# Two scan directions added before one product: ScalarE takes the backward differences, VectorE the sum

## The chip, the cores and the metric

The kernel runs on one core of one Trainium2 chip. The metric is device time in microseconds (us) of one execution, lower is better. The kernel before took 1656.18 us (median of 3 runs, 1655.77 to 1656.74).

## What is computed

A two-layer encoder trunk over 512 positions of width 1024, batch 1, all in float32. Each layer makes one wide projection of the normed input, feeds three mixers (dilated attention, a bidirectional Mamba-2 scan, a short gated convolution), projects their outputs back, and ends in a convolutional feed-forward part. The change touches the scan alone. For one head (16 of them) and one chunk of 128 positions (4 of them) its part within the chunk is, cut to what matters:

```python
a_cs  = cumsum(dt * a)                      # along the chunk
decay = exp(where(lower, a_cs[l] - a_cs[s], -inf))
cb    = einsum(C[l], B[s])                  # shared by the 8 heads of a group
y_diag = (cb * decay) @ (xs * dt)           # 128 x 128 times 128 x 64
y = y_fwd + flip(y_bwd) + d_skip * xs       # two directions, each with its own dt and a
```

The forward direction looks at earlier positions (s <= l), the backward one at later positions, and both use the same B, C and xs.

## The kernel before, in words

**Weights.** All large products go through one stream of weight chunks of 128 x 1024 (list CHUNKS). A chunk is loaded by SyncE (SP) into one of two buffers, split on ScalarE into a rounded high part (`w_high`, L528), and the remainder, the low part, is made by VectorE during the scans (`low_after` of VectorE, L834) or by GpSimd elsewhere (L433). TensorE multiplies high x high, high x low and low x high (L1158 to L1160), 24 products of 512 columns for one tile. The chunk two places further on can be split only when TensorE has used this one, and loaded only when the one before it in the same buffer is split.

**Slots.** While the scans run, each layer steps through 28 slots (list SLOTS, L69): 12 tiles of the short convolution, 8 gate tiles z, 8 tiles of the output projection (o1). Every engine has its own in-order queue, written out by hand with the same loop over the slots, and semaphores tie the queues together. The scans hang on slots by tables: the 16 heads form two groups of 8, the groups begin at slots 2 and 13 (GROUP_AT), SEG_AT says in which slot a head's differences are taken, WEIGH_AT in which it is weighed, PAIR_AT in which a pair of heads (t = 0 to 7, 4 in each group) is multiplied.

**One head.** SP loads the running sums of both directions, spread over all 128 partitions, as one 128 x 2 x 512 tile (`head_rows`, L361; four buffers in turn, called sb_e (two of them), sb_e_third and sb_squares). VectorE subtracts the other position's sum from each chunk and direction and caps at 80: eight instructions of 128 x 128 (`seg`, L905). The column that is subtracted already has ln(dt) in it (L1033). ScalarE takes one Exp over all 128 x 1024 (`head_exp`, L602). VectorE multiplies by the masked products of C and B, which lie in PSUM, 128 x 1024 (`weigh`, L911). For even heads GpSimd adds the two directions, 128 x 512 (`add_directions`, L464).

**One pair.** After the tile of its slot TensorE multiplies the states (`from_states`, L1336, 12 products) and then, in `within` (L1322), takes three products a chunk: one for the even head's sum, two for the odd head's directions, accumulated. The even head writes partitions 0 to 63 of a bank, the odd head 64 to 127. Each float32 product appears as two instructions, so a pair has 24. VectorE's `combine` (L915 to L923) reads them, with the rows that SP's `pair_exps` (L370) loads, and GpSimd adds the backward part (L468) and gates (L473).

**Order around the change.** In a slot VectorE does: `seg`, state work, the tile's own evacuation, `weigh`, `low_after`, `combine`, the rest. ScalarE does `head_exp` before its `w_high` where the head's number within its group is 3 or more, else after it. GpSimd does state scaling, `add_directions`, `add_backward` (L468), gates. SP issues a slot's weight load, then a head's rows, which wait for the products of the pair that used the buffer, then a pair's exps. From slot 18 on, two stretches on ScalarE hold an activation-table change each way around a SiLU (`gate_silu`, L609, L610).

Of the kernel before, what the change touches and what calls it, by code (L numbers as in the profile page):

```python
# [9 lines left out]
ACT, ALU = mybir.ActivationFunctionType, mybir.AluOpType  # L10
P = 128
# [6 lines left out]
SSD_HEADS, SSD_GROUPS = 16, 2  # L18
# [5 lines left out]
QT = SEQ // P  # L24
# [3 lines left out]
DIR = 32  # L28
# [114 lines left out]
def build_trunk(nc, a):  # L143
# [18 lines left out]
    def sem(name, per=0):  # L162
        return Count(ctx.enter_context(nc.semaphore(name)), per, now)
# [16 lines left out]
    SM = sb("small", [P, 4, QT * 64])  # L180
# [51 lines left out]
    def bank(i):  # L232
# [41 lines left out]
    tok_tr, tok_copied = sem("tok_tr", 10), sem("tok_copied", 10)  # L274
    sin_first = sem("sin_first", 4)
    cb_mm, cb_done, xs_done, st_mm, sin_done = sem("cb_mm", 2), sem("cb_done", 4), sem("xs_done", 12), sem("st_mm", 12), sem("sin_done", 8)
    seg_done, e_done, g_done, y_mm = (
        sem(n, SSD_HEADS) for n in ("seg_done", "e_done", "g_done", "y_mm"))
    gs_done = sem("gs_done", SSD_HEADS // 2)
    yo_mm, y_read, t_read, z_copied, y_comb = (sem(n, 8) for n in ("yo_mm", "y_read", "t_read", "z_copied", "y_comb"))  # L280
    z_done = sem("z_done", 2)
    ff_tap, ff_silu, ff_hi, ff_lo = sem("ff_tap", 2 * FF_T), sem("ff_silu_done", FF_T), sem("ff_hi_done", FF_T), sem("ff_lo_done", FF_T)
# [8 lines left out]
    def head_e(h):  # L291

        return HEAD_E[h % 4]
# [9 lines left out]
    def column(d, h):  # L303
        return d * DIR + h
# [120 lines left out]
    def _(pool):  # L425
        g = nc.gpsimd
# [31 lines left out]
            g.tensor_tensor(SQ[:, j % 2, :].rearrange("p (h e) -> p h e", e=64), XT[:, c, :].rearrange("p (h e) -> p h e", e=64),  # L458
                            WS[:, c, col:col + 8].unsqueeze(2).to_broadcast([P, 8, 64]), ALU.mult).then_inc(xs_done.handle, 1)

        def add_directions(h):

            pool.wait_ge(*g_done.at(h + 1))
            g.tensor_tensor(head_e(h)[:, 0, :], head_e(h)[:, 0, :], head_e(h)[:, 1, :], ALU.add).then_inc(gs_done.handle, 1)  # L464

        def add_backward(t):
            pool.wait_ge(*y_read.at(t + 1))
            g.tensor_tensor(XC[:, t, 0:SEQ - P], XC[:, t, 0:SEQ - P], T[:, 1, 0:SEQ - P], ALU.add).then_inc(t_read.handle, 1)  # L468
# [8 lines left out]
        for layer in range(DEPTH):  # L477
            now[0] = layer
            for pos in range(POS["sc", 0]):
                low_after(*CHUNKS[pos])  # L480
                if layer == 0 and CHUNKS[pos] == ("qk", 2):
                    pool.wait_ge(bias_row.handle, 2)
                    g.dma_start(scratch[:, :, :], rm["bias_row"][:, :].unsqueeze(1).to_broadcast([HEADS, COPIES, REL]))\
                        .then_inc(bias_stored.handle, 16)
            for s, (kind, i) in enumerate(SLOTS):
                if kind == "sc" and i % 3 == 2:
                    t = i // 3
                    pool.wait_ge(*sc_hi.at(t + 1))
                    g.tensor_tensor(rm["ml_sc"][:, t, :], SCP[:, :], rm["mh_sc"][:, t, :].bitcast(F32), ALU.subtract)\
                        .then_inc(sc_lo.handle, 1)  # L490
                for grp in range(SSD_GROUPS):
                    if 0 <= s - GROUP_AT[grp] < 3:
                        for j in range(2):
                            scale_states(6 * grp + 2 * (s - GROUP_AT[grp]) + j)
                if s in WEIGH_AT and WEIGH_AT[s] % 2 == 0:
                    add_directions(WEIGH_AT[s])
                if s in PAIR_AT:
                    add_backward(PAIR_AT[s])
                if s in (16, 17):
                    gate(2 * (s - 16))  # L500
                    gate(2 * (s - 16) + 1)
                if s in (20, 21, 22):
                    gate(s - 16)
                if s == 24:
                    gate(7)
                if s in (24, 27):
                    sum_squares((s - 24) // 3)
            for m in range(KT):
                low_after("o2", m)
            for j in range(2 * FF_T):  # L510
                low_after("up", j)
                if j % 2 == 1:
                    t = j // 2
                    pool.wait_ge(*ff_hi.at(t + 1))
                    g.tensor_tensor(FLO[:, t, :], FP[:, :], FHI[:, t, :].bitcast(F32), ALU.subtract).then_inc(ff_lo.handle, 1)  # L515
            for i in range(DOWN_C * KT):
                low_after("dn", i)

    @block.scalar
    def _(act):  # L520
# [77 lines left out]
            sc.activation(PTS[:, u % 4, :, :], bank(4 + u % 2).rearrange("p (j i) -> p j i", i=P), ACT.Copy).then_inc(at_ptc.handle, 1)  # L598

        def head_exp(h):  # L600
            act.wait_ge(*seg_done.at(h + 1))
            sc.activation(head_e(h), head_e(h), ACT.Exp).then_inc(e_done.handle, 1)  # L602

        def gate_silu(last):

# [188 lines left out]
    def _(dve):  # L794
# [34 lines left out]
        def low_after(kind, i):  # L829

            n = now[0] * NCH + POS[kind, i] + 2
            dve.wait_ge(w_hi.handle, n + 1)
            dve.wait_ge(w_lo.handle, n)
            v.tensor_tensor(WLO[:, n % 2, :], W[:, n % 2, :], WHI[:, n % 2, :].bitcast(F32), ALU.subtract).then_inc(w_lo.handle, 1)  # L834
# [64 lines left out]
        def seg(h):  # L899
            dve.wait_ge(*rows_landed[h % 4].at(16 * (h // 4 + 1)))  # L900

            for d in range(2):
                for c in range(QT):
                    at = slice(P * c, P * c + P)
                    ins = v.tensor_scalar(head_e(h)[:, d, at], head_e(h)[:, d, at], AS[:, c, column(d, h):column(d, h) + 1], 80.0,  # L905
                                          ALU.subtract, ALU.min)
            ins.then_inc(seg_done.handle, 1)

        def weigh(h):
            dve.wait_ge(*e_done.at(h + 1))  # L910
            v.tensor_tensor(head_e(h), head_e(h), CB[:, :, :], ALU.mult).then_inc(g_done.handle, 1)  # L911

        def combine(t):
            dve.wait_ge(*y_mm.at(2 * t + 2))
# [27 lines left out]
        for layer in range(DEPTH):  # L942
# [81 lines left out]
            for s, (kind, i) in enumerate(SLOTS):  # L1024
# [4 lines left out]
                if s == 1:  # L1029
                    dve.wait_ge(*cs_tr.at(1))  # L1030
                    dve.wait_ge(*lndt_done.at(1))
                    for d in range(2):
                        step(v.tensor_tensor(AS[:, :, DIR * d:DIR * d + DIR], BANK[:, 3, P * d:P * d + P].rearrange("p (c n) -> p c n", n=DIR),  # L1033
                                             SM[:, 2, :].rearrange("p (c n) -> p c n", n=64)[:, :, DIR * d:DIR * d + DIR], ALU.subtract))
                    dve.sem_inc(cs_col.handle, 1)
                if s in SEG_AT:
                    seg(SEG_AT[s])
                for grp in range(SSD_GROUPS):
# [27 lines left out]
                if s in WEIGH_AT:  # L1066
                    weigh(WEIGH_AT[s])
                low_after(kind, i)
                if s in PAIR_AT:
                    combine(PAIR_AT[s])  # L1070
                if kind == "sc" and i % 3 == 1:
# [75 lines left out]
    def _(pe):  # L1147
# [162 lines left out]

        def within(t):

            pe.wait_ge(*gs_done.at(t + 1))
            pe.wait_ge(*g_done.at(2 * t + 2))
            if t % 4 == 0:
                pe.wait_ge(*cb_done.at(2 * (t // 4) + 2))
            if t >= 2:
                pe.wait_ge(*y_read.at(t - 1))
            for c in range(QT):
                for h, d in ((2 * t, 0), (2 * t + 1, 0), (2 * t + 1, 1)):  # L1320
                    half = 64 * (h % 2)
                    ins = mm(BANK[half:half + 64, 6 + t % 2, P * c:P * c + P], XT[:, c, 64 * (h % 8):64 * (h % 8) + 64],  # L1322
                             head_e(h)[:, d, P * c:P * c + P], start=d == 0, stop=d == h % 2)
                    if c == QT - 1 and d == h % 2:
                        ins.then_inc(y_mm.handle, 1)

        def from_states(t):
# [231 lines left out]
```

## Time and profile before

| | |
|---|---|
| median of 3 runs | 1656.18 us (1655.77 to 1656.74) |
| the profiled execution: its own time | 1656.37 us |
| its span, first to last instruction | 1654.6 us |
| TensorE busy | 1634.1 us, 99% |
| VectorE / ScalarE / GpSimd busy | 993.3 / 661.9 / 674.2 us |
| granted TensorE clock | 1.0 throughout |

Busy time of an engine is the time in which at least one of its instructions ran; matmuls overlap one another, so a busy TensorE can still have shorter work. The scans of the two layers lie at about 217 to 406 us and 1035 to 1224 us. "Idle before" in brackets is how long the engine sat before an instruction, and the releaser is what ended it.

### The profile page before, as it was taken

The page shows a single profiled execution, that of the slowest core. Times are in us where ns is not written, and L with a number is a line of the kernel's source. Part 1 is how long each engine was busy: PE and PEld are TensorE (multiplying, and loading weights), DVE is VectorE, ACT ScalarE, POOL GpSimd, SP SyncE. Part 2 cuts the span into 40 slices and gives each one's busy share as a digit, 9 for nine tenths or more (in the row PEclk, how much of TensorE's full clock was granted, in tenths as well). Part 3 has the DMA queues.
Part 4 walks back from the last instruction along what each step waited for, and adds up shares of the span by engine and source line. Part 5 has one row for each costly group of instructions (what it writes and reads, how often), then busy time and mean ns, then how long its engine had stood idle before and what let it go on. Part 6 is the DMA issues. An engine that isn't in the chain of part 4 may idle for free.

```text
span 1654.6 us, 20299 instructions
## 1 busy us (share of the span) xinstructions
PE 1634.1 (99%) x7864; PEld 1297.6 (78%) x7864; DVE 993.3 (60%) x1564; ACT 661.9 (40%) x916; POOL 674.2 (41%) x339
## 2 busy tenths in 40 slices
PE   7999999999999999999999999999999999999999
PEld 5777778877878888888877777787878788888887
DVE  4589869787764455522227898798887554554000
ACT  5455552335343333332244555523443433333221
POOL 3332222233445555554443222223244555555443
PEclk9999999999999999999999999999999999999999
DMA  5532135442222222222224221444522223222223
GB/s 170 139 91 74 60 117 146 134 146 94 90 90 99 93 91 100 89 92 96 92 90 127 87 74 62 124 146 130 149 95 90 90 89 100 92 91 98 95 92 109
DMA packets 57375, 170.93 MB, mean 103 GB/s; under 512 B 5984, under 2 KB 11872, under 8 KB 57280
## 3 DMA queue, kind: packets, MB, share of 16 engines
q1 hardware_dynamic: 56896, 168.88, 32.1%
q0 software_dynamic: 384, 0.75, 0.4%
q8 instruction: 63, 1.03, 0.3%
q14 instruction: 32, 0.26, 0.1%
HBM read 166.24 MB, written 3.38 MB: 103 GB/s over the span
## 4 chain that ended last, share of the span: by engine, by line
PE 92%; issue 2%; DVE 2%; POOL 1%; DMA 1%; ACT 1%; SPq 0%; DVEq 0%; POOLq 0%; ACTq 0%
PE banks L1158 27%; PE banks L1160 27%; PE banks L1159 27%; PE banks L1257 2%; PE banks L1236 2%; PE banks L1245 2%; PE banks L1322 1%; PE banks L1309 1%; PE banks L1336 1%; DMA sb_w_raw<-w_out 1%; PE banks L1216 1%; DVE sb_h_lo L809 0%; POOL sb_xc L473 0%; PE banks L1293 0%; DVE sb_squares L822 0%
## 5 line engine op out<-in xcount | busy, mean ns | idle before, releaser
L433 POOL TENSOR_TENSOR sb_w_lo<-sb_w_raw,sb_w_hi 128x1024 fp32r<-128x1024 f32 x200 | 482.4, 2412 | 634.9 <-ACT sb_w_hi L528 634.9
L1158 PE MATMUL banks<-sb_h_hi,sb_w_hi 128*128 128x512 f32 x1344 | 550.9, 410 | 11.3 <-POOL sb_w_lo L433 9.9
L528 ACT ACTIVATE sb_w_hi<-sb_w_raw 128x1024 fp32r<-128x1024 f32 x256 | 270.9, 1058 | 706.9 <-PE banks L1160 691.4
L1160 PE MATMUL banks<-sb_h_hi,sb_w_lo 128*128 128x512 f32 x1344 | 530.9, 395 | 0.0
L1159 PE MATMUL banks<-sb_h_lo,sb_w_hi 128*128 128x512 f32 x1344 | 530.6, 395 | 0.0
L1158 PEld LDWEIGHTS banks<-sb_h_hi,sb_w_hi 128*128 128x128 f32 x1344 | 253.5, 189 | 92.4 <-issue 34.7
L1159 PEld LDWEIGHTS banks<-sb_h_lo,sb_w_hi 128*128 128x128 f32 x1344 | 253.8, 189 | 60.9 <-issue 6.5
L1160 PEld LDWEIGHTS banks<-sb_h_hi,sb_w_lo 128*128 128x128 f32 x1344 | 253.5, 189 | 59.4
L1123 DVE TENSOR_TENSOR banks<-banks,sb_rstd 128x512 f32<-128x512 f32 x88 | 61.5, 699 | 145.3 <-PE banks L1160 135.7
L1160 PE MATMUL banks<-sb_ff_hi,sb_w_lo 128*128 128x512 f32 x352 | 138.9, 395 | 0.0
L1159 PE MATMUL banks<-sb_ff_lo,sb_w_hi 128*128 128x512 f32 x352 | 138.9, 395 | 0.0
L1158 PE MATMUL banks<-sb_ff_hi,sb_w_hi 128*128 128x512 f32 x352 | 138.9, 395 | 0.0
L1138 DVE TENSOR_TENSOR sb_x_stream<-banks,sb_x_stream 128x512 f32<-128x512 f32 x16 | 11.1, 692 | 199.2 <-PE banks L1160 199.2
L834 DVE TENSOR_TENSOR sb_w_lo<-sb_w_raw,sb_w_hi 128x1024 fp32r<-128x1024 f32 x56 | 82.1, 1465 | 19.4 <-ACT sb_w_hi L528 19.3
L1158 PEld LDWEIGHTS banks<-sb_ff_hi,sb_w_hi 128*128 128x128 f32 x352 | 66.3, 188 | 15.5
L1159 PEld LDWEIGHTS banks<-sb_ff_lo,sb_w_hi 128*128 128x128 f32 x352 | 66.3, 188 | 15.5
L1160 PEld LDWEIGHTS banks<-sb_ff_hi,sb_w_lo 128*128 128x128 f32 x352 | 66.3, 188 | 15.4
L515 POOL TENSOR_TENSOR sb_ff_lo<-sb_ff_prod,sb_ff_hi 128x512 fp32r<-128x512 f32 x44 | 57.0, 1296 | 51.4 <-DVE sb_ff_hi L1134 51.4
L857 DVE SCALAR_TENSOR_TENSOR sb_xc<-banks,sb_params,sb_xc 128x509 f32<-128x509 f32 (+2 forms) x96 | 71.9, 749 | 4.5 <-ACT sb_xc L585 1.7
L591 ACT ACTIVATE sb_probs<-sb_scores,sb_neg_max 128x512 f32<-128x512 f32 x64 | 45.7, 716 | 57.2 <-DVE sb_neg_max L883 57.2
L1125 DVE SCALAR_TENSOR_TENSOR sb_ff_val<-banks,sb_params,sb_ff_val 128x511 f32<-128x511 f32 x44 | 33.0, 749 | 46.3 <-ACT sb_ff_val L775 46.3
L1125 DVE SCALAR_TENSOR_TENSOR sb_ff_gate<-banks,sb_params,sb_ff_gate 128x511 f32<-128x511 f32 x44 | 33.0, 750 | 45.8 <-ACT sb_ff_gate L775 45.8
(202 smaller groups left out, 2255.9 us busy)
## 6 DMA issues: line engine op xcount, KB each, us to landing
sb_w_raw<-w_in SPq DMA_DIRECT2D x88, 512.0 KB, 3.4
sb_w_raw<-w_up SPq DMA_DIRECT2D x88, 512.0 KB, 3.3
sb_w_raw<-w_out SPq DMA_DIRECT2D x32, 512.0 KB, 3.3
sb_w_raw<-w_down SPq DMA_DIRECT2D x32, 512.0 KB, 3.3
sb_e<-sum_rows SPq DMA_DIRECT2D x16, 512.0 KB, 6.2
sb_bias_t<-bias_rows SPq DMA_DIRECT2D x16, 448.0 KB, 5.6
sb_exp_cs<-sum_rows SPq DMA_DIRECT2D x32, 192.0 KB
sb_w_raw<-w_down SPq DMA_DIRECT2D x16, 384.0 KB, 3.0
```

The lines of the kernel that those rows point to most:

```text
L433: g.tensor_tensor(WLO[:, n % 2, :], W[:, n % 2, :], WHI[:, n % 2, :].bitcast(F32), ALU.subtract).then_inc(w_lo.handle, 1)
L515: g.tensor_tensor(FLO[:, t, :], FP[:, :], FHI[:, t, :].bitcast(F32), ALU.subtract).then_inc(ff_lo.handle, 1)
L528: sc.activation(WHI[:, n % 2, :], W[:, n % 2, :], ACT.Copy).then_inc(w_hi.handle, 1)
L591: sc.activation(PR[:, u % 4, :], S[:, u % 2, :], ACT.Exp, bias=NEGMAX[:, u % 4:u % 4 + 1], scale=-1.0, accum_out=DEN[:, u % 4:u % 4 + 1]). ...
L834: v.tensor_tensor(WLO[:, n % 2, :], W[:, n % 2, :], WHI[:, n % 2, :].bitcast(F32), ALU.subtract).then_inc(w_lo.handle, 1)
L857: ins = v.scalar_tensor_tensor(acc[:, lo:hi], src[:, lo + o:hi + o], par(PA_CONV7 + 8 * n + t), acc[:, lo:hi], ALU.mult, ALU.add)
L1123: v.tensor_tensor(bank(b), bank(b), RSTD, ALU.mult).then_inc(up_scaled.handle, 1)
L1125: step(v.scalar_tensor_tensor(acc[:, 1:SEQ], BANK[:, b, 0:SEQ - 1], par(col), acc[:, 1:SEQ], ALU.mult, ALU.add))
L1158: mm(out, whi, hhi, start=start, stop=False)
L1159: mm(out, whi, hlo, start=False, stop=False)
L1160: return mm(out, wlo, hhi, start=False, stop=stop)
L1236: ins = mm(bank(2 + u % 2), qs[hs, h // 2, P * qt:P * qt + P], ks[hs, h // 2, :], start=n == 0, stop=n == 2)
```

## The change

ScalarE makes the backward direction by itself. It waits for the head's rows, takes Relu(column - row) for the four chunks in place, waits for its own four results, takes Exp(-that + ln dt) for the four chunks, each with a per-partition bias column, and then, when VectorE has the forward differences, Exp over 128 x 512. VectorE's `seg` keeps the four forward instructions. The backward columns are stored without ln(dt). `add_directions` moves from GpSimd, where it ran for even heads, to VectorE, where it runs for all 16, behind `low_after` and ahead of `combine`. `within` takes one product a head and chunk, 16 instructions for a pair, and waits for the sum of the pair's odd head.

```diff
-    seg_done, e_done, g_done, y_mm = (
-        sem(n, SSD_HEADS) for n in ("seg_done", "e_done", "g_done", "y_mm"))
-    gs_done = sem("gs_done", SSD_HEADS // 2)
+    seg_done, gap_done, e_done, g_done, y_mm = (
+        sem(n, SSD_HEADS) for n in ("seg_done", "gap_done", "e_done", "g_done", "y_mm"))
+    gs_done = sem("gs_done", SSD_HEADS)
...
-        def add_directions(h):
-
-            pool.wait_ge(*g_done.at(h + 1))
-            g.tensor_tensor(head_e(h)[:, 0, :], head_e(h)[:, 0, :], head_e(h)[:, 1, :], ALU.add).then_inc(gs_done.handle, 1)
...
-                if s in WEIGH_AT and WEIGH_AT[s] % 2 == 0:
-                    add_directions(WEIGH_AT[s])
...
         def head_exp(h):
+            if h == 0:
+                act.wait_ge(*cs_col.at(1))
+                act.wait_ge(*lndt_done.at(1))
+            act.wait_ge(*rows_landed[h % 4].at(16 * (h // 4 + 1)))
+
+            for d in (1,):
+                for c in range(QT):
+                    at, col = slice(P * c, P * c + P), column(d, h)
+                    ins = sc.activation(head_e(h)[:, d, at], head_e(h)[:, d, at], ACT.Relu, bias=AS[:, c, col:col + 1], scale=-1.0)
+            ins.then_inc(gap_done.handle, 1)
+            act.wait_ge(*gap_done.at(h + 1))
+            for d in (1,):
+                for c in range(QT):
+                    at, col = slice(P * c, P * c + P), 64 * c + column(d, h)
+                    ins = sc.activation(head_e(h)[:, d, at], head_e(h)[:, d, at], ACT.Exp, bias=SM[:, 2, col:col + 1], scale=-1.0)
             act.wait_ge(*seg_done.at(h + 1))
-            sc.activation(head_e(h), head_e(h), ACT.Exp).then_inc(e_done.handle, 1)
+            sc.activation(head_e(h)[:, 0, :], head_e(h)[:, 0, :], ACT.Exp).then_inc(e_done.handle, 1)
...
-            for d in range(2):
-                for c in range(QT):
-                    at = slice(P * c, P * c + P)
-                    ins = v.tensor_scalar(head_e(h)[:, d, at], head_e(h)[:, d, at], AS[:, c, column(d, h):column(d, h) + 1], 80.0,
-                                          ALU.subtract, ALU.min)
+            for c in range(QT):
+                at = slice(P * c, P * c + P)
+                ins = v.tensor_scalar(head_e(h)[:, 0, at], head_e(h)[:, 0, at], AS[:, c, column(0, h):column(0, h) + 1], 80.0,
+                                      ALU.subtract, ALU.min)
             ins.then_inc(seg_done.handle, 1)
...
+        def add_directions(h):
+
+            dve.wait_ge(*g_done.at(h + 1))
+            v.tensor_tensor(head_e(h)[:, 0, :], head_e(h)[:, 0, :], head_e(h)[:, 1, :], ALU.add).then_inc(gs_done.handle, 1)
...
-                    for d in range(2):
-                        step(v.tensor_tensor(AS[:, :, DIR * d:DIR * d + DIR], BANK[:, 3, P * d:P * d + P].rearrange("p (c n) -> p c n", n=DIR),
-                                             SM[:, 2, :].rearrange("p (c n) -> p c n", n=64)[:, :, DIR * d:DIR * d + DIR], ALU.subtract))
-                    dve.sem_inc(cs_col.handle, 1)
+                    step(v.tensor_tensor(AS[:, :, 0:DIR], BANK[:, 3, 0:P].rearrange("p (c n) -> p c n", n=DIR),
+                                         SM[:, 2, :].rearrange("p (c n) -> p c n", n=64)[:, :, 0:DIR], ALU.subtract))
+                    v.tensor_copy(AS[:, :, DIR:2 * DIR], BANK[:, 3, P:2 * P].rearrange("p (c n) -> p c n", n=DIR))\
+                        .then_inc(cs_col.handle, 1)
...
                 if s in WEIGH_AT:
                     weigh(WEIGH_AT[s])
                 low_after(kind, i)
+                if s in WEIGH_AT:
+                    add_directions(WEIGH_AT[s])
                 if s in PAIR_AT:
                     combine(PAIR_AT[s])
...
-            pe.wait_ge(*gs_done.at(t + 1))
-            pe.wait_ge(*g_done.at(2 * t + 2))
+            pe.wait_ge(*gs_done.at(2 * t + 2))
...
             for c in range(QT):
-                for h, d in ((2 * t, 0), (2 * t + 1, 0), (2 * t + 1, 1)):
+                for h in (2 * t, 2 * t + 1):
                     half = 64 * (h % 2)
                     ins = mm(BANK[half:half + 64, 6 + t % 2, P * c:P * c + P], XT[:, c, 64 * (h % 8):64 * (h % 8) + 64],
-                             head_e(h)[:, d, P * c:P * c + P], start=d == 0, stop=d == h % 2)
-                    if c == QT - 1 and d == h % 2:
+                             head_e(h)[:, 0, P * c:P * c + P], start=True, stop=True)
+                    if c == QT - 1:
                         ins.then_inc(y_mm.handle, 1)
```

## Rows read from the trace of the kernel before

**Rows 1.** The page, part 1: busy us (share of the span), instructions.
```profile
PE 1634.1 (99%) x7864; PEld 1297.6 (78%) x7864; DVE 993.3 (60%) x1564; ACT 661.9 (40%) x916; POOL 674.2 (41%) x339
```

**Rows 2.** Waits of TensorE: us in total, times, longest us.
```profile
PE banks L1322 <- issue: 3.2, 4, 1.2
PE banks L1158 <- DVE sb_z L1085: 1.8, 2, 1.0
```

**Rows 3.** Chain in order of time: start us, us, what.
```profile
110.11 1.02 PE banks L1257 x16
...
262.10 1.90 PE banks L1322 x24
```

**Rows 4.** Busy us by stretch: PE, PEld, DVE, ACT, POOL, clock, DMA share, GB/s.
```profile
250.00:282.00 32.00, 32.00 (x178) 26.01 (x178) 30.20 (x53) 9.87 (x11) 6.86 (x5) 1.00 0.50 143
```

**Rows 5.** Groups of instructions, shapes apart: busy, mean ns | idle before, releaser.
```profile
L905 DVE TENSOR_SCALAR sb_e<-sb_e,sb_small 128x128 f32<-128x128 f32 x128 | 37.5, 363 | 0.1
L905 DVE TENSOR_SCALAR sb_squares<-sb_squares,sb_small 128x128 f32<-128x128 f32 x64 | 25.5, 469 | 0.1
L905 DVE TENSOR_SCALAR sb_e_third<-sb_e_third,sb_small 128x128 f32<-128x128 f32 x64 | 14.1, 292 | 0.1
L609 ACT ACT_TABLE_LOAD x4 | 5.1, 1283 | 8.5 <-DVE sb_z L1085 8.5
```

**Rows 6.** Single lines: duration ns minimum/median/maximum, first and last start.
```profile
L651 ACT ACTIVATE sb_params<-sb_params x2: 241/241/241, 84.1 to 902.3; 128x64 f32<-128x64 f32 x2
L591 ACT ACTIVATE sb_probs<-sb_scores,sb_neg_max x64: 706/718/727, 99.2 to 1018.4; 128x512 f32<-128x512 f32 x64
L556 ACT ACTIVATE sb_rstd<-sb_rstd x6: 632/632/634, 23.1 to 1292.5; 128x512 f32<-128x512 f32 x6
```

**Rows 7.** VectorE in order of time, slots 4 to 8: start us, us, instruction, [idle before].
```profile
251.18 1.22 DVE L834 TENSOR_TENSOR sb_w_lo<-sb_w_raw,sb_w_hi 128x1024 fp32r<-128x1024 f32 x1
252.32 2.57 DVE L1076 SCALAR_TENSOR_TENSOR sb_sc_acc<-sb_sc_cx,sb_params,sb_sc_acc 128x511 f32<-128x511 f32 x2
254.92 1.66 DVE L905 TENSOR_SCALAR sb_e_third<-sb_e_third,sb_small 128x128 f32<-128x128 f32 x8
...
257.82 0.68 DVE L937 TENSOR_TENSOR sb_t_normed<-sb_s_in,sb_decays 128x512 f32<-128x512 f32 x1
...
260.48 1.21 DVE L911 TENSOR_TENSOR sb_e<-sb_e,banks 128x1024 f32<-128x1024 f32 x1
261.61 2.05 DVE L834 TENSOR_TENSOR sb_w_lo<-sb_w_raw,sb_w_hi 128x1024 fp32r<-128x1024 f32 x1
...
274.71 1.53 DVE L1076 SCALAR_TENSOR_TENSOR sb_sc_acc<-sb_sc_cx,sb_params,sb_sc_acc 128x511 f32<-128x511 f32 x2
```

**Rows 8.** VectorE in order of time, slots 9 to 22.
```profile
295.20 2.35 DVE L834 TENSOR_TENSOR sb_w_lo<-sb_w_raw,sb_w_hi 128x1024 fp32r<-128x1024 f32 x1
...
385.00 4.52 DVE L905 TENSOR_SCALAR sb_squares<-sb_squares,sb_small 128x128 f32<-128x128 f32 x8
```

**Rows 9.** GpSimd in order of time.
```profile
251.34 2.21 POOL L464 TENSOR_TENSOR sb_e<-sb_e 128x512 f32<-128x512 f32 x1 [1.63 <-DVE sb_e L911]
261.30 1.27 POOL L489 TENSOR_TENSOR sb_ml_sc<-sb_sc_prod,sb_mh_sc 128x512 fp32r<-128x512 f32 x1 [7.75 <-ACT sb_mh_sc L699]
...
384.50 1.46 POOL L468 TENSOR_TENSOR sb_xc<-sb_xc,sb_t_normed 128x384 f32<-128x384 f32 x1 [1.35 <-DVE sb_xc L923]
385.92 2.54 POOL L473 TENSOR_TENSOR sb_xc<-sb_xc,sb_z 128x512 f32<-128x512 f32 x2
```

**Rows 10.** ScalarE in order of time.
```profile
271.34 1.06 ACT L602 ACTIVATE sb_squares<-sb_squares 128x1024 f32<-128x1024 f32 x1 [9.17 <-DVE sb_squares L905]
...
363.54 1.06 ACT L528 ACTIVATE sb_w_hi<-sb_w_raw 128x1024 fp32r<-128x1024 f32 x1 [1.74 <-DMA sb_w_raw<-w_out]
...
378.56 1.04 ACT L602 ACTIVATE sb_e_third<-sb_e_third 128x1024 f32<-128x1024 f32 x1
```

**Rows 11.** TensorE in order of time: the first product of pair 7.
```profile
391.97 0.29 PE L1322 MATMUL banks<-sb_e_third,sb_x_tok 128*64 128x128 f32 x1 [1.20 <-issue]
```

## The prediction

> **What bounds the kernel now.** I read the page's busy times first: TensorE has an instruction running in 1634.1 of 1654.6 us [rows 1], so work taken from it counts, and any other engine matters only where it makes TensorE wait. The waits of TensorE show that the scans cost it little now: four waits ahead of L1322, 3.2 us together, and two ahead of a projection tile for the last gate tile's evacuation, 1.8 us [rows 2]. The chain in order of time then gives the price of what the change shortens: the 24 instructions of a pair take 1.90 us, and the attention's L1257, with the same shape (128 rows, 64 columns, 128 moving), 16 of them alternating between the two partition halves, takes 1.02 us [rows 3]. Last come the stretches and the timelines of the other engines: in one stretch of 32 us within the scans VectorE is busy for 30.2 us, ScalarE for 9.87, GpSimd for 6.86 [rows 4]. VectorE is the second limit, close behind TensorE, and the change makes TensorE wait for one more VectorE instruction in every pair.
>
> **The change part by part.** *Products.* A pair goes from 24 instructions to 16, alternating between the halves. By the same-shaped row it takes 1.02 instead of 1.90 us: 0.88 less, 16 pairs in two layers, 14.1 us [rows 3]. Were the halves not to overlap better, 16/24 of 1.90 is 1.27 and the saving 10.1. I take 1.02, as the shape and the alternation are the same. This is gain only where the pair's operands are ready.
>
> *Differences on VectorE.* Eight instructions become four. All 256 cost 37.5 + 25.5 + 14.1 = 77.1 us [rows 5], so 38.5 us go. Undisturbed, eight take 1.66 us [rows 7], four 0.83; but a batch can last 4.52 us [rows 8], where GpSimd works through 1.46 + 2.54 us beside it [rows 9], and then half the batch may not last half as long.
>
> *The sum on VectorE.* The nearest row is a 128x512 two-input operation on SBUF of 0.68 us, of which about 0.08 overlaps the next one [rows 7]: 0.60 us, 32 times, 19 us. Beside GpSimd it may cost 1.27 more, the length of a GpSimd operation [rows 9]; less than 0.60 is excluded, since the elements are the same. VectorE is so relieved by some 19 us, but the relief lies ahead of the weighing and the new work behind it: between the weighing of a pair's odd head and TensorE's start there now stand the weight split (1.22 us alone, 1.14 from its start to the next one's, 2.05 beside GpSimd [rows 7]) and the sum, at least 1.74 us that were not there.
>
> *ScalarE.* A 64-column activation takes 0.241 us and a 512-column one 0.632; between them 128 columns take 0.30. A bias column adds 0.718 - 0.632 = 0.09 [rows 6]. Four take about 1.26 us (0.09 of each under the next), four Relu and four Exp 2.43 with the wait between, and the Exp of 512 columns 0.6: 3.05 us against 1.06, 64 us more over both layers. The new wait on its own Relu costs 0.03 to 0.1 and holds only what ScalarE does next. Mostly it is free: ScalarE sits up to 9.17 us waiting for VectorE's differences [rows 10], and the 2.43 us go into that time, because they need the rows alone; then the Exp that is left is 0.43 us shorter. Where it isn't free is head 14: there ScalarE comes from the SiLU with its table changes and starts its Exp at 378.56 the moment it can [rows 10]; the 2.43 us go on the path. No table change is added: Copy, Square and Exp stand side by side now without one, and I take Relu to be like them (bounds below).
>
> *GpSimd, SP, the column in L1033.* GpSimd loses its 16 sums, one of them 2.21 us [rows 9]; this frees VectorE where they met: two taps took 2.57 us beside one, 1.53 alone [rows 7]. SP's order and DMAs are the same; a head's rows wait for the pair that frees their buffer, so the loads behind them move with the pairs. The copy in place of one subtraction lies in a stretch where VectorE waits for TensorE; I take it as nothing, and at worst one operation a layer, 0.3 us.
>
> *The pairs, one by one (layer 0; layer 1 repeats it).* Pair 0: VectorE reaches the weighing of head 1 at 260.48 [rows 7]. Before it the taps lose 1.04 and the differences 0.83, the sum of head 0 adds 0.60: 1.27 earlier. The weight split that ended at 263.66 ends at 262.4, still beside GpSimd [rows 7, 9], the new sum at 263.05. TensorE stood ready at 262.10 - 0.07 = 262.03 [rows 3]: it waits 1.0 us, saves 0.88, and ends 0.15 later. Pair 1 has its sums in time: 0.88 earlier, -0.75 in all. Pair 2: the split before it hangs on a weight load that doesn't move; the two sums add 1.20, the split that now lies in between 1.14, the differences and the Exp give back 1.3; TensorE waits 0.6 and stands at -1.05, or at 0 where the sum meets GpSimd's operation. Pair 3 waited 0.4 before (of the four waits, 3.2 in all, two are of 1.2 [rows 2]); the split at 295.20 loses its disturbance by a GpSimd sum (2.35 to 1.22 [rows 7, 8]), its load comes 0.7 earlier, differences -0.83, two sums +1.20, split +1.14: -1.13 - 0.7 - 0.83 + 1.20 + 1.14 moves the start by -0.3 and, with the product, the end by -1.2, or by -0.1 where the split meets GpSimd. I take the middle: -0.65 at the end of the first group.
>
> Pairs 4 and 5: in time, -0.88 each. But the tile behind them already waits for the gate tile's evacuation [rows 2], which stands behind a weight split held up by a load (1.74 us of idle at 363.54 [rows 10]). That load follows pair 4 and comes 0.88 earlier, one sum adds 0.60: of -1.76 only -0.3 is left. Pair 6: -1.2. Pair 7 began at 391.97 after a wait of 1.20 [rows 11]. ScalarE gets there 1.6 earlier (-0.3, head 13's differences -0.83, its Exp -0.43), but the 2.43 us come on top and only 0.43 goes: head 14's Exp ends 0.4 later. Its sum adds 0.60, so the last batch of differences starts 1.0 later; GpSimd's 4.0 us [rows 9] move with it, so the batch of four ends 0.25 later than the eight did. Then Exp -0.43, split +1.14, sum +0.60: the start is 1.56 later and the end, 0.88 sooner after it, 0.7 later; were the batch half of 4.52, the end would be 0.8 earlier than now. I take +0.2, nearer the end at which GpSimd's work moves along.
>
> *Sum.* -0.65 + 0.2 = -0.45 a layer, -0.9 in all, against 14.1 us of saved products: TensorE gives back in new waits nearly all that it saves. From the profiled execution's own 1656.37 (span 1654.6 and 1.8 around it) this is 1655.5; that execution is 0.19 above the median, so **1655.3 us**. The ends of the forecast: -1.2 - 0.8 = -2.0 a layer, 1652.2; and -0.1 + 0.7, with one meeting of sum and GpSimd more in each group (1.27 each), +3 a layer, 1662, where the slower rival lies.
>
> A rule speaks against the Relu on ScalarE. The row says: VectorE's four differences take 0.83 us alone, my estimate for ScalarE's four is 1.26 [rows 6, 7]. The Trainium skill, ScalarE: Activation LUTs, section Rules for kernel authors, says to give relu to VectorE and not to ScalarE. By that rule the Relu would be 1.26 us of pure loss at head 14, the one place where ScalarE is late; without it pair 7 would end near -1 and the sum would be about 1653. The trace gives the rule no force elsewhere, since ScalarE idles there.
>
> **The rivals.** *VectorE gets ahead (faster).* For it: 38.5 us of differences go and 19 us of sums come, and GpSimd's share of the port falls. If this clears every pair but the fourth of each group and the gate tile, first groups give 3 x 0.88 + 0.4, second groups 2 x 0.88 + 0.3, about 5 a layer: 1646; with all 14.1, 1642. Against it: the relief lies ahead of the weighing, and weight loads, which don't move, set the start in three of the waits.
>
> *The sums meet GpSimd (slower).* Place: slots 8, 11, 16 and 22, where VectorE's new sum or the split before it starts while GpSimd holds an operation of 1.27 to 2.54 us. It decides where GpSimd starts first: the split at 261.61 ran 2.05 us beside a GpSimd operation begun at 261.30, the one at 251.18 took 1.22 [rows 7, 9]. Two such meetings on the path of each group, 1.27 us each, are 5 a layer: 1655.3 + 10 = 1665, half of it 1660. Against it: GpSimd's own 16 sums are gone. Beside this stands the Trainium skill, GPSIMD Engine Reference, section Key points: GpSimd shares its SBUF interfaces with VectorE, which bears on VectorE instructions with two SBUF inputs; the trace agrees by the 2.05 against 1.22 us.
>
> *ScalarE is late.* If Relu asked for a table change each way, 1.28 us each by the SiLU's [rows 5], a head would cost 2.6 more on ScalarE, and at three heads a group on the path some 15 in all each layer: about 1685. I see no Relu in the trace. The Trainium skill, ScalarE: Activation LUTs, section Table sets, says relu is in every set; by that no change is added.
>
> *The change doesn't do what it says.* The pair's 16 instructions could stay at 1.27; since TensorE then waits less, this moves the sum by under 2 us, within the forecast.
>
> **How the numbers follow.** A difference of 0.2%, 3.3 us, is about what a measurement of this kernel can tell from no change. Forecast, a balance within 3.3 us: 0.46. VectorE ahead: 0.31. Sums that meet GpSimd: 0.18. ScalarE late: 0.05. So faster 0.31, same 0.46, slower 0.23. The forecast's own range is 1652.9 to 1659.5, the median of the runs and 3.3 either way; its far ends above count with the rivals. The range goes from 1647 (most of the first rival) to 1661 (half of the second).
>
> **What would show it.** Right: a pair of 16 instructions near 1.0 us; L1322 waits grown from 3.2 us to some 12 or more, mainly at pairs 0, 3 and 7 of each layer; the gate tile's wait near 5 us; batches of differences halved where GpSimd is silent; ScalarE's Relu and Exp of 128 columns near 0.39 us, with no table loads beside them; the sum near 0.68. Wrong: waits of L1322 that don't grow (then near 1645), sums of 1.3 to 2 us ahead of pairs, or weight tiles (L1158) that wait for the low part in the scans.

## The result, and the profile after

The changed kernel takes 1664.48 us (median of 6 runs, 1662.46 to 1665.14) against 1656.16 us for the kernel before (6 runs): ratio 1.0046, 95% interval 1.0036 to 1.0056, that is 8.3 us or 0.5% slower. The forecast was 1655.3, the range ended at 1661. The profiled execution took 1665.14 us with a span of 1663.4, 8.8 more than before; its mean granted TensorE clock is 0.995, where it was 1.000.

The page's busy times answer to [rows 1]:

```profile
PE 1627.5 (98%) x7736; PEld 1288.9 (77%) x7736; DVE 973.7 (59%) x1468; ACT 725.8 (44%) x1172; POOL 641.7 (39%) x323
```

Each engine moved as the parts of the forecast said: VectorE is 20 us less busy, ScalarE 64 us more, GpSimd 33 us less. TensorE has 128 instructions fewer, yet its busy time fell by only 6.6 us where 14 were removed. Its waits, the answer to [rows 2] (line waited at, what ended the wait; us in total, times, longest):

```profile
PE banks L1335 <- DVE sb_squares L923: 8.8, 4, 3.8
PE banks L1335 <- DVE sb_e L923: 5.8, 4, 2.2
PE banks L1172 <- DVE sb_z L1099: 4.8, 2, 2.5
```

L1335 is `within`, L923 the new sum, L1099 the evacuation of the last gate tile. The waits of the scans grew from 5.0 us to 19.4, by 14.4. The operations themselves have the sizes of the forecast (groups with shapes apart: busy us, mean ns, idle before):

```profile
L602 ACT ACTIVATE sb_e<-sb_e,sb_small 128x128 f32<-128x128 f32 x64 | 20.3, 388 | 0.3 <-DMA sb_e<-sum_rows 0.3
L608 ACT ACTIVATE sb_e<-sb_e,sb_small 128x128 f32<-128x128 f32 x64 | 20.5, 391 | 0.5
...
L923 DVE TENSOR_TENSOR sb_e<-sb_e 128x512 f32<-128x512 f32 x16 | 13.1, 820 | 0.0
L923 DVE TENSOR_TENSOR sb_squares<-sb_squares 128x512 f32<-128x512 f32 x8 | 5.5, 683 | 0.0
```

What the forecast had no term for stands in the windows around pair 2 of layer 0 (length of the window in us; busy us of PE, PEld, DVE, ACT, POOL with instructions; then the granted clock, DMA share, GB/s):

```profile
292.00:294.00 2.00, 0.26 (x3) 0.06 (x1) 2.00 (x3) 1.97 (x7) 0.00 (x0) 1.00 0.14 50
294.00:296.00 2.00, 1.58 (x17) 1.25 (x17) 1.90 (x7) 1.44 (x4) 0.00 (x0) 0.70 0.65 217
296.00:298.00 2.00, 2.00 (x7) 1.62 (x6) 1.41 (x2) 1.43 (x2) 0.00 (x0) 0.50 0.29 113
298.00:300.00 2.00, 2.00 (x10) 1.61 (x9) 2.00 (x3) 1.97 (x7) 0.00 (x0) 0.94 0.13 48
300.00:302.00 2.00, 2.00 (x11) 1.60 (x10) 1.90 (x5) 0.82 (x3) 0.00 (x0) 1.00 0.99 257
```

and in TensorE's timeline of the same stretch (start, us, what, idle before):

```profile
294.42 1.64 PE L1335 MATMUL banks<-sb_e,sb_x_tok 128*64 128x128 f32 x16 [2.17 <-DVE sb_e L923]
295.99 0.80 PE L1172 MATMUL banks<-sb_h_hi,sb_w_hi 128*128 128x512 f32 x1
296.58 0.63 PE L1173 MATMUL banks<-sb_h_lo,sb_w_hi 128*128 128x512 f32 x1
297.01 0.63 PE L1174 MATMUL banks<-sb_h_hi,sb_w_lo 128*128 128x512 f32 x1
...
298.51 0.39 PE L1172 MATMUL banks<-sb_h_hi,sb_w_hi 128*128 128x512 f32 x1
298.74 0.39 PE L1173 MATMUL banks<-sb_h_lo,sb_w_hi 128*128 128x512 f32 x1
```

After a wait of 2.17 us the granted clock fell from 1.00 (2.4 GHz) to 0.50 (1.2 GHz): the pair took 1.64 us, and a product of 512 columns started every 0.43 us in place of every 0.23, until the clock came back before 298.5. The same is seen behind the gate tile (a wait of 2.51 us) and pair 7 (2.44) of layer 0, and pair 7 of layer 1 (3.81).

Summed over windows of 2 us through both scans, the time that the clock was short of, (1 - granted clock) x 2 us, is 8.6 us, all of it in 13 windows at these four places. The same sum is nothing in the kernel before.

### The profile page after: what moved, and what is told of

Same layout as the page of the kernel before. It is cut to its first block, busy times and chain, and to the rows that moved or that the text cites. A ratio compares the mean times of both kernels' runs of the same rounds, so it can differ in the third digit from the quotient of the medians.

```text
span 1663.4 us, 20183 instructions
## 1 busy us (share of the span) xinstructions
PE 1627.5 (98%) x7736; PEld 1288.9 (77%) x7736; DVE 973.7 (59%) x1468; ACT 725.8 (44%) x1172; POOL 641.7 (39%) x323
## 4 chain that ended last, share of the span: by engine, by line
PE 85%; DVE 6%; DMA 5%; ACT 2%; issue 2%; SPq 0%; DVEq 0%; ACTq 0%
PE banks L1172 26%; PE banks L1174 25%; PE banks L1173 25%; DMA sb_w_raw<-w_in 3%; PE banks L1271 2%; PE banks L1250 2%; DMA sb_w_raw<-w_out 2%; PE banks L1259 2%; DVE sb_w_lo L842 1%; PE banks L1323 1%; PE banks L1230 1%; PE banks L1335 1%; DVE sb_squares L912 1%; ACT sb_w_hi L521 1%; DVE sb_h_lo L817 0%
## 5 line engine op out<-in xcount | busy, mean ns | idle before, releaser
L1172 PE MATMUL banks<-sb_h_hi,sb_w_hi 128*128 128x512 f32 x1344 | 551.5, 410 | 12.3 <-POOL sb_w_lo L433 10.8
L842 DVE TENSOR_TENSOR sb_w_lo<-sb_w_raw,sb_w_hi 128x1024 fp32r<-128x1024 f32 x56 | 75.0, 1340 | 30.2 <-ACT sb_w_hi L521 30.2
L463 POOL TENSOR_TENSOR sb_xc<-sb_xc,sb_t_normed 128x384 f32<-128x384 f32 x16 | 18.9, 1178 | 136.9 <-DVE sb_xc L935 136.9
```

The lines of the kernel that those rows point to most:

```text
L1172: mm(out, whi, hhi, start=start, stop=False)
```

## The experiments

The theory after this reading (A): the saved products are given back as waits, and the longer waits cost a second time, because TensorE runs at half the clock for some us after them. Rivals: the waits alone are the loss; or the work on ScalarE is. Beside each set of runs the kernel before took 1656.3 to 1656.9 us.

**The sum first.** In a slot the sum stands right behind the weighing, ahead of the weight split.

```diff
                 if s in WEIGH_AT:
                     weigh(WEIGH_AT[s])
+                    add_directions(WEIGH_AT[s])
                 low_after(kind, i)
-                if s in WEIGH_AT:
-                    add_directions(WEIGH_AT[s])
```

> The changed kernel with one edit: VectorE takes the sum right behind the weighing, ahead of the weight split. Theory A (TensorE waits because split and sum both stand between weighing and pair, and its granted clock falls to half only after the longest of those waits): waits ahead of a pair fall from 14.6 us to 4 to 6, those for the gate tile stay near 2 each, mean granted clock 0.998 or more, time 1647 to 1652, faster than the kernel before. Theory B (ScalarE's ten instructions a head, or GpSimd on the shared port, make the sums late): the waits shrink by less than 0.6 us each, 1660 or more. Theory C (the clock falls because a pair now has 16 instructions, whatever it waits): clock stays at 0.995 and the time near 1656.

Measured: 1658.36 us (10 runs), ratio 1.0007 [0.9997, 1.0016]. That is 6.1 us better than the change, less than was expected: the waits ahead of pairs are 8.9 us, not 4 to 6, and the time lies over the range of 1647 to 1652. Pairs 0 and 2 no longer wait, so there the place of the sum was the cause. Pairs 3 and 7 still wait 2.2 us each. At pair 3 the sum now meets GpSimd (VectorE, then GpSimd, in order of time):

```profile
303.83 1.21 DVE L918 TENSOR_TENSOR sb_squares<-sb_squares,banks 128x1024 f32<-128x1024 f32 x1
305.07 1.52 DVE L923 TENSOR_TENSOR sb_squares<-sb_squares 128x512 f32<-128x512 f32 x1
```

```profile
304.79 1.26 POOL L484 TENSOR_TENSOR sb_ml_sc<-sb_sc_prod,sb_mh_sc 128x512 fp32r<-128x512 f32 x1 [3.67 <-ACT sb_mh_sc L707]
```

and the gate tile's evacuation still waits behind split and combine (4.1 us in two waits). At the end of the scans 2.6 us of waits for GpSimd's sum of squares are new.

**TensorE kept busy in the waits.** 18 products of 512 columns, 0.86 us each, whose results nobody reads, are issued ahead of the long waits of pairs 2, 3 and 7 and the gate tile: the waits stay, the idle time in them mostly goes.

```diff
+            fill(6 + t % 2, {2: 2, 3: 2, 7: 3}.get(t, 0))
...
+                if (kind, i) == ("o1", 1):
+                    pe.wait_ge(*y_read.at(5))
+                    fill(6, 2)
```

> The changed kernel with products that nobody reads (ones times constants, 128x512, 0.86 us each) put ahead of the waits of pairs 2, 3 and 7 (2, 2, 3 of them) and of the tile that waits for the gate tile (2): 18 in two layers, 15.5 us more work for TensorE, the other engines' work the same. Theory A (the waits are set by VectorE and the clock falls because TensorE stands still in them): the waits shrink by what fills them, the clock stays at 1.000 and the time falls by the clock's share, to 1655 to 1659, with 15.5 us more work. Theory C (clock not tied to the waits): 1664 to 1668. If the waits were not really idle time that can be filled: 1680.

Measured: 1660.62 us (9 runs), ratio 1.0024 [1.0014, 1.0034], over theory A's range of 1655 to 1659; the clock is 1.000, so the 16 instructions of a pair do not lower it by themselves (theory C). The waits that are left:

```profile
PE banks L1340 <- DVE sb_squares L923: 3.2, 4, 1.2
PE banks L1340 <- DVE sb_e L923: 2.9, 4, 1.0
...
PE banks L1172 <- DVE sb_z L1099: 1.0, 2, 0.5
```

With 18 x 0.86 = 15.5 us more work for TensorE the kernel is 3.9 us faster than the change. Idle time and fill come to 7.1 + 15.5 = 22.6 us here, against 19.4 us of waits in the change, so what went is the stretches at half clock. Their net price is thus some 4 us of the 8.3; the other 4 are the waits themselves.

**ScalarE's part alone.** ScalarE's Relu and biased Exp stay; the sums go back to GpSimd for even heads, and three products a chunk are taken as before.

```diff
-            pe.wait_ge(*gs_done.at(2 * t + 2))
+            pe.wait_ge(*gs_done.at(t + 1))
+            pe.wait_ge(*g_done.at(2 * t + 2))
...
-                for h in (2 * t, 2 * t + 1):
+                for h, d in ((2 * t, 0), (2 * t + 1, 0), (2 * t + 1, 1)):
```

> ScalarE's part of the change alone: Relu and biased Exp for the backward direction, four differences on VectorE; GpSimd's sums for even heads and three products a chunk as in the kernel before. Theory A: VectorE is relieved and nothing is put behind its weighing, so the waits ahead of a pair go from 3.2 us to under 1.5, ScalarE is not late but at pair 7, clock 1.000, time 1651 to 1655. Theory B (ScalarE late): waits at pairs 2, 3, 7 as in the changed kernel, 1660 or more.

Measured: 1654.95 us (10 runs), ratio 0.9988 [0.9978, 0.9998] against 1656.85 us of before, 1.9 us better. ScalarE's 64 us more of work cost the kernel nothing that shows: of the pairs only pair 7 still waits, 0.8 us in each layer.

```profile
PE banks L1336 <- issue: 1.7, 2, 0.8
PE banks L1172 <- DVE sb_z L1099: 1.3, 2, 0.7
```

**The sums and the single product alone.** VectorE takes all eight differences and all sums; ScalarE keeps one Exp over 128 x 1024.

```diff
-            sc.activation(head_e(h)[:, 0, :], head_e(h)[:, 0, :], ACT.Exp).then_inc(e_done.handle, 1)
+            sc.activation(head_e(h), head_e(h), ACT.Exp).then_inc(e_done.handle, 1)
...
-            for c in range(QT):
+            for d in range(2):
+                for c in range(QT):
```

> The other part alone: sums of all heads on VectorE and one product a head and chunk, with eight differences on VectorE and one Exp of 128x1024 on ScalarE as in the kernel before. Theory A: VectorE carries 19 us of sums more and is relieved of nothing: the waits grow to 25 us or more, clock 0.985 to 0.993, time 1675 to 1695. Theory B (the loss is ScalarE's): without its part the saved products come through, 1645 to 1653.

Measured: 1672.76 us (one run), clock 0.994; the waits of the scans come to 24.1 us. The time is 2 us short of theory A's range, the waits are just under its 25 us, and theory B is out:

```profile
PE banks L1321 <- DVE sb_e L909: 10.3, 4, 3.4
PE banks L1321 <- DVE sb_squares L909: 9.3, 4, 2.9
PE banks L1158 <- DVE sb_z L1085: 4.5, 2, 2.3
```

So the loss belongs to the sum on VectorE in TensorE's path (+15.9 us with the shorter pairs already in it), and the differences on ScalarE win back half of it.

**Head 14's Relu on VectorE.** Four more differences there; ScalarE makes only that head's exponentials.

```diff
-            act.wait_ge(*gap_done.at(h + 1))
+            if h == 14:
+                act.wait_ge(*seg_done.at(h + 1))
...
+            for c in range(QT if h == 14 else 0):
+                at = slice(P * c, P * c + P)
+                ins = v.tensor_scalar(head_e(h)[:, 1, at], head_e(h)[:, 1, at], AS[:, c, column(1, h):column(1, h) + 1], 0.0,
                                       ALU.subtract, ALU.min)
```

> The changed kernel, but head 14's backward differences are made by VectorE (four more subtract-and-cap instructions behind the forward four), and ScalarE makes only its four biased exponentials and the Exp of 512 columns. All other heads stay. Theory A (at pair 7 ScalarE is late: it leaves the SiLU behind time and its four Relu, 1.26 us, stand on the path): the wait ahead of pair 7's products falls from 2.44 us (layer 0) and 3.81 us (layer 1) by about 0.8 to 1.3 each, at least one of the two stretches at half the granted clock behind them goes, all other waits stay; time 1659 to 1662. Rival B (pair 7 waits for the differences of head 15, stretched beside GpSimd, whenever they start): four more VectorE instructions change nothing or add to it; waits at pair 7 stay within 0.4 us or grow, time 1664 to 1666.

**GpSimd's gates held back.** Gates 5 and 6 wait for the sum of head 15.

```diff
-                if s in (20, 21, 22):
-                    gate(s - 16)
+                if s == 20:
+                    gate(4)
+                if s == 22:
+                    pool.wait_ge(*gs_done.at(16))
+                    gate(5)
+                    gate(6)
```

> The changed kernel, but GpSimd's gates 5 and 6 (two operations each of 128x512) wait until VectorE has summed head 15, so that they don't run beside head 15's differences. Nothing else. Theory A (GpSimd's operations stretch these four differences from 0.87 to 3.74 us): the four take 0.9 to 1.6 us (one GpSimd operation, the backward part, still lies near them), the wait ahead of pair 7 falls by 2 us or more each layer to under 1.5 us, the clock stays full there, time 1657 to 1661. Rival B (the differences are long for another reason, or pair 7 waits for ScalarE all the same): the four stay over 3 us or the wait stays over 2 us; time 1663 to 1666.

Measured: 1660.44 us (10 runs), ratio 1.0022 [1.0012, 1.0031], with head 14's Relu moved; 1659.42 us (10 runs), ratio 1.0017 [1.0007, 1.0026], with the gates held. Both times lie where theory A had them. The waits at pair 7 are a poor measure, since TensorE too comes at another time: 2.44 and 3.81 us (layer 0, layer 1) became 2.71 and 2.69 with the Relu moved, where 0.8 to 1.3 less was expected, and 1.71 and 1.72 with the gates held, where under 1.5 was. The other places did not stay as they were either: with the Relu moved no stretch at half clock is left behind pair 7, nor behind pair 2 and the gate tile of layer 0, but new ones stand behind pair 3 of layer 0 and pair 2 of layer 1. What is the same in both layers is the distance from the first table load of the SiLU on ScalarE to pair 7's first product: in the change 22.2 us (374.56 to 396.79), with the Relu moved 20.9 (375.05 to 395.97), with the gates held 20.1 (375.00 to 395.12). The two ends in the change (ScalarE, then TensorE):

```profile
374.56 1.28 ACT L617 ACT_TABLE_LOAD   x1
```

```profile
396.79 0.32 PE L1335 MATMUL banks<-sb_e_third,sb_x_tok 128*64 128x128 f32 x1 [2.44 <-DVE sb_squares L923]
```

So at this place ScalarE's four Relu cost 1.3 us and GpSimd's two gates 2.1. The gates act through head 15's differences; in the change (VectorE, then GpSimd):

```profile
389.34 3.74 DVE L912 TENSOR_SCALAR sb_squares<-sb_squares,sb_small 128x128 f32<-128x128 f32 x4
```

```profile
388.83 1.46 POOL L463 TENSOR_TENSOR sb_xc<-sb_xc,sb_t_normed 128x384 f32<-128x384 f32 x1 [9.63 <-DVE sb_xc L935]
390.26 2.54 POOL L468 TENSOR_TENSOR sb_xc<-sb_xc,sb_z 128x512 f32<-128x512 f32 x2
```

and with the gates held:

```profile
389.78 1.63 DVE L916 TENSOR_SCALAR sb_squares<-sb_squares,sb_small 128x128 f32<-128x128 f32 x4
```

Four such differences take 0.87 us where GpSimd is silent. Here they end 0.28 us after GpSimd's last operation (393.08 against 392.80), and in windows of 0.2 us one gives way to the next at 390.3 to 390.5, 391.5 to 391.7 and 392.7 to 392.9, each time where an operation of GpSimd ends. The Trainium skill, SBUF — State Buffer, section "SBUF: two separate sides", calls the port pair of VectorE and GpSimd an exclusive lock and not a split of bandwidth; the trace agrees by these ends.

**Both orders.** The sum first, gates 5 and 6 behind head 15's sum, GpSimd's product of slot 11 behind head 7's sum, the last gate tile's evacuation ahead of split and combine; on ScalarE the first square and high part of the scan's output one slot later.

```diff
+                    if t == 3:
+                        pool.wait_ge(*gs_done.at(8))
...
+                    add_directions(WEIGH_AT[s])
+                if (kind, i) == ("z", 7):
+                    dve.wait_ge(*w_used.at(POS[kind, i] + 1))
+                    dve.wait_ge(*y_comb.at(i - 3))
+                    v.tensor_tensor(Z[:, i % 4, :], bank(b), RSTD, ALU.mult).then_inc(evac[b].handle, 1)
                 low_after(kind, i)
```

> The changed kernel with the sum right behind the weighing (as in the run with the sum first), GpSimd's gates 5 and 6 behind the sum of head 15, its product of the short convolution in slot 11 behind the sum of head 7, the last gate tile's evacuation ahead of the weight split and the combine of its slot, and in slot 21 the first tile's square and high part behind head 14's exponentials on ScalarE. Theory A (the 14.1 us of products are there for whoever takes the waits away; all of them are matters of order): waits of TensorE in the scans under 6 us in all, granted clock 1.000, time 1641 to 1649, faster than both kernels. Rival B (VectorE has too much work ahead of each pair, so that a wait taken away in one place comes back in the next): waits in the scans stay over 12 us, time 1654 to 1659.

Measured: 1655.69 us (11 runs), ratio 0.9994 [0.9985, 1.0003]; rival B's numbers, with 13.7 us of waits left. Pairs 0, 1, 2 and the gate tile don't wait, and pair 7 starts at 388.39, before its 391.97 [rows 11]; but the waits have come back behind it:

```profile
PE banks L1233 <- POOL sb_sq_ssd L448: 7.4, 2, 3.7
PE banks L1184 <- DVE sb_w_lo L851: 3.4, 2, 2.1
PE banks L1347 <- DVE sb_squares L932: 2.9, 2, 1.4
```

The largest is not in the place that B named, VectorE's work ahead of a pair, but at the end of the scan: the combine of pair 7, the gate and the sum of squares, once hidden because TensorE came later. Behind these 3.7 us the clock fell again:

```profile
404.00:408.00 4.00, 3.34 (x6) 2.02 (x7) 2.48 (x3) 1.19 (x2) 0.61 (x1) 0.50 0.44 131
```

**Orders again.** In addition, head 15's differences, a weight split and the combine of pair 6 use an idle stretch of 4.1 us that VectorE had ahead of head 14's weighing, the combine of pair 7 goes ahead of other work, and head 7's sum ahead of an evacuation.

```diff
+                if s == 21:
+                    seg(15)
+                    low_after(kind, i)
+                    combine(6)
...
+                if s == 22:
+                    combine(7)
+                if s == 10:
+                    seg(7)
```

> The kernel with both orders changed, and in addition: head 15's differences, the weight split of slot 21 and the combine of pair 6 go into VectorE's idle stretch ahead of head 14's weighing; on ScalarE that slot's high part stands ahead of head 14's Relu, and the scan output's squares and high parts behind head 15's exponentials; the combine of pair 7 stands in slot 22 and the low parts behind it; head 7's differences go ahead of the taps of slot 10, and its weighing and sum ahead of that slot's evacuation. Theory A (the waits left over are three places of order: the split of slot 21 with 2.1 and 1.3 us, pair 3 with 1.4 us, the sum of squares behind the late combine of pair 7 with 3.7 us, in each layer or one of them): they fall from 15 to under 4 us in all, the granted clock is 1.000, and the time is 1638 to 1646, beyond what a measurement can take for no change against both kernels. Rival B (the waits are worth only their idle time and come back elsewhere in VectorE's queue): over 8 us of waits in the scans are left, time 1649 to 1655.

Measured: 1646.78 us (5 runs, 1645.04 to 1647.73), ratio 0.9939 [0.9925, 0.9953] to the kernel before: 9.6 us faster than it and 17.7 faster than the change, the clock 1.000 again. The time is 0.8 us over the range of theory A and 2.2 under that of B; of waits 7.8 us are left, twice what A allowed. The waits that are left, none over 1.5 us:

```profile
PE banks L1193 <- DVE sb_w_lo L848: 7.3, 8, 1.5
...
PE banks L1356 <- DVE sb_squares L929: 0.5, 2, 0.3
```

## Why the prediction was wrong

**The sum is the step that failed**: "-0.45 a layer, -0.9 in all, against 14.1 us of saved products: TensorE gives back in new waits nearly all that it saves". Two of its terms were too low. Each wait entered it at its idle time, with nothing for a lower clock behind it. And the end of the first group was put at -0.65 a layer, the middle between a meeting with GpSimd and none, where both meetings took place. On the spans, beside them the run in which TensorE was kept busy and the clock stayed full (its waits are idle time and fill):

| term | forecast | the change | TensorE kept busy |
|---|---|---|---|
| products, 16 pairs | -14.1 | -13.9 (an undisturbed pair 1.03 for 1.90) | -13.9 |
| waits in the scans | +13.2 | +14.4 | +17.6 |
| longest wait for the first weights | none | +0.9 | +0.2 |
| half clock behind long waits | none | +7.4 (the rest) | +0.9 (the rest, at full clock) |
| sum | -0.9 | +8.8 | +4.8 |

The rest of 7.4 us is close to what the clock says: 0.5% of 1663.4 us is 8.3, and the windows give 8.6. Not all of that could be had back, since a TensorE that comes later waits less at the next place: kept busy, the kernel won 3.9. So of the 9.7 us between forecast and measurement some 4.0 are the net price of the half clock, of which the clock column of before, 1.00 throughout, gave no sign, and 4.4 are waits that were put too low; the other 1.3 are small terms. That the waits of the change itself lie within 1.2 us of the forecast is luck: the late TensorE hid the difference. Pair 3 shows how: it waits 0.39 us in layer 0, where the clock had fallen at pair 2, and 2.17 in layer 1, where it had not. The longest wait for the first weights was 9.9 us before and 10.1 to 10.8 in every other kernel here; its cause was not looked for.

**The pairs, one by one.** At full clock (idle time and fill) pair 0 waits 1.0 us a layer, pair 2 some 2.2, pair 3 some 2.1, the gate tile 2.2 and pair 7 3.8. The second group, 2.2 + 3.8 less 2.1 of waits before and 3.5 of products, so ends 0.4 later, forecast 0.2: right. Pair 0 and the gate tile are right as well (1.0, and near 5 together). The first group, 1.0 + 2.2 + 2.1 less 0.4 and 3.5, ends 1.4 later and not 0.65 sooner. The two meetings with GpSimd, which the forecast had written down as its other ends, are as large as this 2.0. At pair 2 the sum of head 4 lasted 1.78 us for 0.68, at pair 3 the weight split 2.21 for 1.22; the change, layer 0 (VectorE, then GpSimd):

```profile
284.94 1.78 DVE L923 TENSOR_TENSOR sb_e<-sb_e 128x512 f32<-128x512 f32 x1
...
307.30 2.21 DVE L842 TENSOR_TENSOR sb_w_lo<-sb_w_raw,sb_w_hi 128x1024 fp32r<-128x1024 f32 x1
```

```profile
284.36 1.80 POOL L484 TENSOR_TENSOR sb_ml_sc<-sb_sc_prod,sb_mh_sc 128x512 fp32r<-128x512 f32 x1 [13.01 <-ACT sb_mh_sc L707]
...
307.13 1.30 POOL L484 TENSOR_TENSOR sb_ml_sc<-sb_sc_prod,sb_mh_sc 128x512 fp32r<-128x512 f32 x1 [3.67 <-ACT sb_mh_sc L707]
```

Layer 1 repeats both (1.79 and 2.18 us). What they cost TensorE is read from these lengths. A run bears on it at pair 3 alone: there GpSimd's product put behind the sum took the wait from 2.25 us (the sum first) to 1.43 (both orders).

Pair 7 is later by the two things that were named, ScalarE's Relu (estimated at 1.26, measured 1.3) and GpSimd beside the differences; "the batch of four" does last about as long as GpSimd's 4.0 us. The distance from the table load, 22.2 us, was 19.1 before (372.89 to 391.97 [rows 11]): 3.1 more, and the forecast's 1.6 sooner at ScalarE and 1.56 later at pair 7 make 3.2.

```profile
372.89 1.28 ACT L609 ACT_TABLE_LOAD   x1
```

**The rivals.** "The sums meet GpSimd" was right in mechanism and came true by less than half: two meetings in each first group and none in the second, 2 x (1.1 + 1.0) = 4.2 us for its 10; of the 32 sums only two were long. "ScalarE is late" fell: no table change came, and ScalarE's part alone is faster than before. "VectorE gets ahead" fell for this order of the work, but its 1646 is what the last run reached: the relief was there, at the wrong side of the weighing.

**The rule on relu.** The forecast kept it out of the sum but for head 14. The runs bear that out: at head 14 VectorE's Relu saves 1.3 us a layer by the distances (4.0 in all, with what changed in the stretches at half clock elsewhere), but with all of the backward differences on VectorE the kernel is 8.3 us slower than the change (one run). The Trainium skill, ScalarE: Activation LUTs, section Rules for kernel authors, sends relu to VectorE by the engines' speeds; here the queue that is waited for decides.

## What to carry to other kernels

Saving work on the bound engine by putting one more instruction of another engine ahead of it can be worth nothing while that instruction stands behind other work in its queue. Move the sum right behind its operand, and what nobody waits for behind it: here that gave 6.1 us, and it took the order of all that stands ahead of TensorE to gain 17.7. When TensorE's new waits come to some 2 us each, read the granted clock by short windows as well, since the loss can go on after the wait is over; and when one wait is taken away, look at what stood ready behind it, as the end of the scan here.

## What the runs showed of the hardware

The length of a wait did not decide by itself whether the clock fell. Behind 2.17 us (pair 2) and 2.44 us (pair 7) it went to half, and in the run with the sums and the single product alone already behind 1.77 us (pair 3 of layer 0):

```profile
314.00:316.00 2.00, 2.00 (x9) 1.52 (x6) 1.84 (x4) 0.00 (x0) 0.00 (x0) 0.63 0.94 232
316.00:318.00 2.00, 2.00 (x6) 1.60 (x5) 1.32 (x3) 0.00 (x0) 1.01 (x1) 0.52 0.95 261
```

But behind 2.71 us at pair 7, in the run with head 14's Relu on VectorE, it stayed, and the pair's products last 0.27 us:

```profile
392.00:396.00 4.00, 1.29 (x14) 1.10 (x12) 3.90 (x7) 3.71 (x6) 0.00 (x0) 1.00 0.02 6
396.00:400.00 4.00, 4.00 (x29) 3.31 (x30) 3.93 (x6) 1.08 (x2) 0.00 (x0) 1.00 0.53 163
```

In the change itself pair 3 and the gate tile of layer 1 waited 2.17 and 2.24 us without a fall. What makes the difference wasn't found. The kernels whose waits lie there scatter more: the ten runs with that Relu moved lie between 1658.04 and 1662.72 us, with mean clocks of 0.996 to 0.999, where those of ScalarE's part alone, all at 1.000, lie between 1653.94 and 1655.77.
